# Later scores and value weighing in TensorE's order, and early low passes in the out sections

## The reference

```python
h = h + rmsnorm(mixer(rmsnorm(h, g_pre)), g_post)      # mixer: gated MLP with short convolution, then dilated attention
h = h + rmsnorm(squared_relu_mlp(rmsnorm(h, ...)), ...) # 2048 -> 8192 -> 2048
# second block, each of two layers:
proj = rms_norm(x, pre_w) @ w_in
y_a = diff_attention(...)                # 4 heads
y_b = sliding_window_attention(...)      # 16 heads
qc = (rms_norm(c_q, q_norm_w) @ w_uq)    # latent heads: 4 heads,
kvc = (rms_norm(c_kv, kv_norm_w) @ w_ukv)#   q and k/v from 512 latent features
y_c = causal_attention(qc, kc, vc, (128 + 64) ** -0.5)
y = concatenate([y_a, y_b, y_c]) * silu(gates)
x = x + rms_norm(y @ w_out, post_w)
```

## Time and profile before

| | us |
|---|---|
| median of 3 runs | 3119.56 (3118.34 to 3119.57) |
| the profiled execution's own time | 3119.79 |
| its span in the trace | 3118.1 |
| PE busy | 3032.2, 97% |
| DVE busy | 2190.6, 70% |
| ACT busy | 1458.1, 47% |
| mean granted PE clock | 0.989 |

### The profile page before, as it was taken

One profiled execution on the slowest core, in us unless ns is written; L12 is line 12 of the kernel. 1 busy time (PEld: TensorE's weight loads), 2 busy tenths in 40 slices (PEclk: granted clock), 3 DMA queues, 4 the chain that ended last, 5 costly groups with the idle time before them and its releaser, 6 DMA issues. The chain is left out here.

```text
span 3118.1 us, 48135 instructions
## 1 busy us (share of the span) xinstructions
PE 3032.2 (97%) x17715; PEld 2661.8 (85%) x17715; DVE 2190.6 (70%) x2926; ACT 1458.1 (47%) x1842; POOL 284.3 (9%) x191
## 2 busy tenths in 40 slices
PE   8999999999999999999999999999899989999997
PEld 7888888888888888888888888888788878788887
DVE  6876765767666687766856666676879755889664
ACT  5334534434334555545433333345656445656443
POOL 0002300000001400004000000003200004100003
PEclk9999999999999999999999999999999999999999
DMA  6555455555555444444555555555344435344434
GB/s 236 187 178 188 166 189 189 183 194 188 189 189 189 158 173 165 173 162 162 189 189 189 189 188 188 189 189 189 147 178 149 162 119 192 141 176 156 149 135 175
DMA packets 76554, 548.28 MB, mean 176 GB/s; under 512 B 8480, under 2 KB 8992, under 8 KB 10656
## 3 DMA queue, kind: packets, MB, share of 16 engines
q1 hardware_dynamic: 76448, 546.81, 48.4%
HBM read 544.68 MB, written 2.10 MB: 175 GB/s over the span
## 5 line engine op out<-in xcount | busy, mean ns | idle before, releaser
L771 ACT ACTIVATE w_high<-raw 128x2048 fp32r<-128x2048 f32 x506 | 965.5, 1908 | 1103.0 <-DMA raw<-stream 1102.1
L287 PE MATMUL acc<-xs,w_high 128*128 128x512 f32 x4947 | 1247.6, 397 | 15.5 <-ACT w_high L922 9.4
L1190 DVE TENSOR_TENSOR w_low<-raw,w_high 128x2048 fp32r<-128x2048 f32 x506 | 1156.1, 2285 | 97.5 <-ACT w_high L771 94.4
L287 PEld LDWEIGHTS acc<-xs,w_high 128*128 128x128 f32 x4947 | 912.2, 190 | 205.4 <-ACT w_high L922 9.4
L287 PE MATMUL acc<-inner,w_high 128*128 128x512 f32 x2976 | 714.9, 392 | 2.8 <-DVE inner L1276 2.8
L294 PE MATMUL acc<-xs,w_low 128*128 128x256 f32 x4962 | 684.8, 283 | 0.0
L294 PEld LDWEIGHTS acc<-xs,w_low 128*128 128x128 f32 x4962 | 657.1, 192 | 23.8
L287 PEld LDWEIGHTS acc<-inner,w_high 128*128 128x128 f32 x2976 | 547.5, 189 | 109.7 <-DVE inner L1276 3.7
L1209 DVE TENSOR_REDUCE y<-acc 128x256 f32<-128x512 f32 x406 | 280.0, 690 | 497.8 <-PE acc L294 496.6
L294 PEld LDWEIGHTS acc<-inner,w_low 128*128 128x128 f32 x2976 | 381.4, 191 | 14.6
L294 PE MATMUL acc<-inner,w_low 128*128 128x256 f32 x2976 | 385.8, 282 | 0.0
(11 more groups left out here) (163 smaller groups left out, 1388.4 us busy)
## 6 DMA issues: line engine op xcount, KB each, us to landing
raw<-stream SPq DMA_DIRECT2D x514, 1024.0 KB, 4.8
h<-x_t SPq DMA_DIRECT2D x4, 512.0 KB, 8.1
out<-h SPq DMA_DIRECT2D x4, 512.0 KB, 2.6
raw<-stream SPq DMA_DIRECT2D x2, 512.0 KB, 7.3
consts<-tables SPq DMA_DIRECT2D x1, 960.0 KB, 16.0
branch<-w_spatial SPq DMA_DIRECT2D x1, 512.0 KB, 16.8
branch<-b_spatial SPq DMA_DIRECT2D x1, 512.0 KB, 17.6
prob_t<-lambdas SPq DMA_DIRECT2D x1, 256.0 KB, 17.7
```

The lines of the kernel that those rows point to most:

```text
L287: nc.tensor.matmul(acc[s][:, :], w_high[:, s, kt * P:(kt + 1) * P], x[:, kt, :, :], start=(kt == first_of[0]), stop=False, skip_group_chec ...
L771: nc.scalar.activation(w_high[:, s, 0:units * P], raw[:, s, 0:units * P], ACT.Copy)\
L1190: V.tensor_tensor(w_low[:, s, 0:units * P], raw[:, s, 0:units * P], w_high[:, s, 0:units * P], ALU.subtract).then_inc(low_ready, 1)
```

## The change

Three things change, all of them in PE's order. The streams of DVE, ACT, POOL and SP hold the same instructions in the same order, and PE runs the same matmuls.

```diff
@@ product_early: second loop
                 for s in range(3):
+                    pe.wait_ge(low_ready, c + s + 1)
+                    for kt in order[:early]:
+                        low_unit(s, kt, inner, False)
                     for i, kt in enumerate(order[early:]):
                         if s == 0:
                             pe.wait_ge(sem("inner_ready"), split0 + early + i + 1)
                         high_unit(s, kt, inner)
-                    pe.wait_ge(low_ready, c + s + 1)
-                    for kt in range(KB):
-                        mm = low_unit(s, kt, inner, kt == KB - 1)
+                    for kt in order[early:]:
+                        mm = low_unit(s, kt, inner, kt == order[-1])
                     mm.then_inc(product_done, 1)
@@ out section after the dilated heads
-                10: last_dilated_turns, 24: lambda: weigh(HEADS - 1, 1, v_nat, HEADS - 1, v=HEADS - 1)})
+                20: last_dilated_turns, 34: lambda: weigh(HEADS - 1, 1, v_nat, HEADS - 1, v=HEADS - 1)})
@@ latent heads, both layers
-                    hooks = {6: lambda: mla_scores(hd - 1)} if hd else {
+                    hooks = {15: lambda: mla_scores(hd - 1)} if hd else {
...
-                        hooks[2] = lambda: mla_weigh(hd - 2)
+                        hooks[9] = lambda: mla_weigh(hd - 2)
@@ out section after the latent heads
-                    2: lambda: mla_weigh(hd - 1), 6: lambda: mla_scores(hd), 34: lambda: mla_turns(hd),
+                    9: lambda: mla_weigh(hd - 1), 14: lambda: mla_scores(hd), 34: lambda: mla_turns(hd),
```

## The result

The changed kernel takes 3091.86 us (median of 4, 3090.94 to 3092.81) where the kernel before took 3118.95 in the same comparison (3117.4 to 3119.57). The ratio is 0.9912, with a 95% interval of 0.9900 to 0.9924: 27.1 us less, with 3092 forecast. The profiled execution took 3091.55, its span is 3089.8.

What follows compares the result with a forecast made beforehand. PE, busy 3032.2 of 3118.1 us, was taken as the bound, with some 86 us of gaps to win. 2 x (4.8 + 5.3 + 1.6) + 3.95 = 27.35 us off the median 3119.56 gave 3092, range 3088 to 3101.

Steps and rivals of the forecast that it cites:

- The weighing, 1.6 each: Latent heads, weighing from unit 2 to 9: the wait for `prob_t` shrinks from 1.64 to about 0.04 us, six times.
- The first head's scores, 5.3 per layer: First latent head, scores from unit 6 to 15: gain 5.3 us, some 2 idle and 3.3 clock; 0.76 wait stays.
- The other heads' scores, no cost: Other latent heads, scores from unit 6 to 15: 0.7 us of cover, DVE's chain does not move, cost 0.
- The late block, 1.6 per layer: Out sections after the latent heads: low units pulled ahead cover the wait for the late `inner` block, gain 1.6 us.
- The dilated heads, 3.95: Out section after the dilated heads: ten more units before the turns remove their wait, gain 2.25 plus 1.7 us of clock.
- The MLP halves, nothing: Sections without a late-block wait: low pass pulled ahead has 4 us of cover for `w_low`, cost 0.
- A: Latent heads: the clock still falls around the 0.76 us waits; gain only 19.1 us, giving 3100; chance 0.13.
- B: Latent heads: waits only move, to the turns or the scores; six times 1.6 us back, 3102; chance 0.08.
- C: `product_early` sections: pulled-ahead low pass waits for `w_low`, 13 x 2.28 = 29.6 us, giving 3121.8; chance 0.02.
- D: Tails of the 13 `product_early` sections: lower clock for 8 us each costs 52 us, giving 3144; chance 0.01.

Runs made afterwards that it cites:

- the run with unit 12: Changed kernel with the scores of each layer's first latent head at unit 12 instead of 15: 3096.28 us, ratio to the kernel before 0.9930.
- The two runs of the hooks alone: Changed kernel with the low pass order of before, so only scores, weighing and turns moved, run twice: 3097.03 us and 3098.13 us.

## Why the prediction was right

*The weighing, 1.6 each.* The third head's product takes 8.49 us to the latent product (2504.09 to 2512.58) against 10.11: 1.62 won. Counting from start to start rather than by brackets was right; six brackets of 1.40 would have missed 1.3 us.

*The first head's scores, 5.3 per layer.* 2489.32 to 2497.86 is 8.54 us against 13.71: 5.17. The wait that stays was put at 0.76 from start to start and shows as 0.61 idle. The clock stayed up behind it. This was the least certain step, and the run with unit 12 shows how near it was: with 0.7 us more of wait the clock fell in the profiled execution and, by their times, in some of the others. Why 0.76 is short enough no run shows; the forecast had no reason for it but that longer waits had passed.

*The other heads' scores, no cost.* The cover by DVE's order held: 6.89 us before and after. The run with the scores alone, where they end another microsecond later, gained what was reckoned within 0.4 us.

*The late block, 1.6 per layer.* From the weighing to the fourth chunk 9.68 us before (2561.04 to 2570.72) and 8.03 now (2546.38 to 2554.41): 1.65. The two runs of the hooks alone give the low pass order nearly 2 us more than its two waits, and that part isn't explained.

*The dilated heads, 3.95.* The first unit to the fourth chunk took 22.07 us (1369.96 to 1392.03) and takes 18.22 (1369.70 to 1387.92): 3.85. The stretch as a whole gained 4.3, since the clock was also up for longer at the norm behind it. Of the 3.85 only the wait of 2.27 is sure. The clock's part, forecast as 1.7, was read from one execution, and two of the five profiled kernels with this wait don't have the fall; that the whole term came out is in part luck. No run moves these two pieces alone.

*The MLP halves, nothing.* 0.02 us each by the trace of the run that changes them alone.

*The rivals.* A didn't come, B neither: no turn waits for a normalisation. C and D can be laid aside: no low unit waits for `w_low`, and the reordered passes run at 1.00. Their prices rest on a wrong count. The kernel has four out sections, not five, and with the eight MLP halves twelve `product_early` sections, not thirteen. So C would have cost at most 12 x 2.28 = 27.4 us, just what is gained, and not been slower than before; D 48 us. On bank changes the trace doesn't bear out, for this kernel, what the Trainium skill ("TensorE: Matmul & The Clock Gate", section "A second HAM failure mode: psum-queue depth-cycling") warns of, a clock that changes its level where TensorE has short gaps between groups of matmuls in changing PSUM banks. Here the passes follow without a gap (busy 10.00 of 10.00 us from 2546 to 2556), and the clock reads 1.00 in all twelve sections, but for the fall behind the turns of the last dilated head in the kernel before.

*Small errors of the working.* Brackets instead of starts would have made the sum some 2 us smaller, not 3: 0.24 for each of eight waits and 0.16 for the dilated heads'. And that the median came out at the forecast's 3092 to 0.1 us is luck: the executions of the changed kernel alone lie 1.9 us apart.

The sum of the touched stretches, from the rows, is 2 x (3 x 1.62 + 5.17 + 1.65) + 3.85 = 27.2; forecast 27.35. The rest of the 28.2 between the two profiled executions is clock near the norms and the start, where the wait for the first weights is 0.4 us shorter.

## What to carry to other kernels

In an order written by hand, give each piece the time at which its data is ready, counted from the last point where the engines meet, and move it behind as much work as fills that time, no more. Then look whose work ends last: where the other engine has slack up to the next meeting point the wait is won (1.62 of 1.64 us), and where its chain is full the wait comes back at the next piece, and longer. Where pieces wait one after another, move them together or the later one first: the weighing alone cost 20 us, the scores alone gained 10, both together more than the sum. And price a wait of TensorE with the clock: the granted level behind it can cost more than the idle time (3.3 us against 2 at the first head's scores).

## What was not expected of the hardware

The length of a wait doesn't tell whether the clock falls, and neither does the order around it. Waits of 1.40 us idle for `prob_t` left it at the 2.4 GHz level six times out of six in the kernel before; waits of 1.30 in front of the scores brought it to 1.2 GHz in both layers; waits of 2.0 did so three times in one layer of an execution and not once in the other, with the same order of work; and one wait of 2.11, the same in five profiled kernels, brought a fall in three. Each fall seen behind such a wait costs between 1.7 and 3.4 us, and how many come differs between executions of one kernel: those of the run with the weighing alone lie from 3130.1 to 3139.7. What decides it is open. So such a fall is better forecast as a chance than as a fixed price.
